# Block-product projection: raw weights in a buffer of their own, weight work ahead of the shaping, three norms first in the conditioning

## What is computed

```python
mod = silu(c) @ w_ada + b_ada              # 1024 x 3072
shift, scale, gate = split(mod, 3)
h = rms_norm(x, norm_g) * (1 + scale) + shift
u = h @ w_in                               # 1024 x 8192
a_q, a_f, a_i, a_g, b_q, b_k, b_v, b_g = split(u)
o_a = rms_norm(hgrn2(a_q, a_f, a_i)) * silu(a_g)
o_b = rms_norm(stick_breaking(b_q, b_k, b_v)) * silu(b_g)
x = x + gate * (concat(o_a, o_b) @ w_out)
return rms_norm(x) * final_g
```

## Time and profile before

| | us |
|---|---|
| median of 3 runs | 3369.33 |
| lowest and highest | 3368.42, 3372.13 |
| the profiled execution | 3368.01 |
| its span, first to last instruction | 3366.2 |
| TensorE busy | 2992.5 (89%) |
| VectorE busy | 1887.7 (56%) |
| ScalarE busy | 1279.8 (38%) |
| GpSimd busy | 615.1 (18%) |
| conditioning | 0 to 107.4 |
| projection, matmuls | 121.8 to 1661.0 |

### The profile page before, as it was taken

How to read it: one execution, slowest core, us unless ns; L and a number is a source line. 1 busy time by engine, 2 the same in 40 slices (tenths; PEclk the granted TensorE clock), 3 DMA queues, 4 the chain that set the end, 5 groups by cost and what they waited for, 6 DMA issues and landing times. The chain is left out here.

```text
span 3366.2 us, 50012 instructions
## 1 busy us (share of the span) xinstructions
PE 2992.5 (89%) x19104; PEld 2509.7 (75%) x19104; DVE 1887.7 (56%) x2013; ACT 1279.8 (38%) x2090; POOL 615.1 (18%) x384
## 2 busy tenths in 40 slices
PE   6687889999687888999888885999999999979998
PEld 4566667777576667878688885887887888868887
DVE  2644334444643334343388884887888878754343
ACT  3422222333323222333211112777777777731111
POOL 0221122222311122222166552000000000000000
PEclk8798899999898898999899997999999999989999
DMA  8124444333323444333344434444243441053220
GB/s 319 38 88 118 129 117 119 97 98 99 108 88 110 131 113 128 100 98 100 122 146 142 135 101 117 111 126 127 51 108 96 126 118 35 14 181 121 79 100 38
DMA packets 277208, 369.72 MB, mean 110 GB/s; under 512 B 13680, under 2 KB 194160, under 8 KB 268272
## 3 DMA queue, kind: packets, MB, share of 16 engines
q1 hardware_dynamic: 276496, 366.03, 35.6%
q10 hardware_dynamic: 480, 0.53, 0.1%
HBM read 244.87 MB, written 121.64 MB: 109 GB/s over the span
## 5 line engine op out<-in xcount | busy, mean ns | idle before, releaser
L470 PE MATMUL b_ps<-hc_hi,w_hi 128*128 128x512 f32 x1792 | 526.9, 418 | 188.9 <-DVE w_lo L581 164.9
L470 PEld LDWEIGHTS b_ps<-hc_hi,w_hi 128*128 128x128 f32 x1792 | 339.6, 198 | 273.9 <-DVE w_lo L581 185.1
L650 DVE TENSOR_TENSOR u<-b_ps,u 128x512 f32<-128x512 f32 x320 | 220.5, 689 | 516.7 <-PE b_ps L470 516.3
L470 PE MATMUL b_ps<-hc_lo,w_hi 128*128 128x512 f32 x1792 | 506.5, 406 | 0.0
L470 PE MATMUL b_ps<-hc_hi,w_lo 128*128 128x512 f32 x1792 | 495.1, 399 | 0.0
L1341 DVE TENSOR_TENSOR_SCAN run<-akeep 128x768 f32<-128x768 f32 (+7 forms) x256 | 414.1, 1660 | 130.4 <-ACT akeep L1311 129.6
L470 PEld LDWEIGHTS b_ps<-hc_lo,w_hi 128*128 128x128 f32 x1792 | 354.4, 198 | 80.0
L470 PEld LDWEIGHTS b_ps<-hc_hi,w_lo 128*128 128x128 f32 x1792 | 349.2, 195 | 78.5
L501 ACT ACTIVATE w_hi<-w_raw 128x1024 fp32r<-128x1024 f32 (+1 forms) x192 | 216.0, 1190 | 409.8 <-POOL w_raw L320 409.8
L1300 ACT ACTIVATE wt<-t_ps 128x512 f32<-128x512 f32 (+3 forms) x640 | 313.5, 534 | 143.6 <-PE t_ps L1230 143.4
L1230 PE MATMUL t_ps<-ident,run 128*128 128x128 f32 x2176 | 311.5, 278 | 7.7 <-DVE run L1341 7.0
(11 more groups left out here) (151 smaller groups left out, 3514.4 us busy)
## 6 DMA issues: line engine op xcount, KB each, us to landing
w_raw<-in_w_in SPq DMA_DIRECT2D x128, 512.0 KB, 4.8
aq<-s_qhi SPq DMA_DIRECT2D x64, 256.0 KB, 6.1
aq<-s_qlo SPq DMA_DIRECT2D x64, 256.0 KB, 6.6
o<-s_o SPq DMA_DIRECT2D x16, 1024.0 KB, 5.9
ada<-in_w_ada SPq DMA_DIRECT2D x12, 1024.0 KB, 9.1
xg<-in_x SPq DMA_DIRECT2D x4, 2048.0 KB, 12.7
s_gq<-u SPq DMA_DIRECT2D x32, 256.0 KB, 2.5
s_gf<-u SPq DMA_DIRECT2D x32, 256.0 KB, 2.5
```

The source lines that it names most:

```text
L470: mm = nc.tensor.matmul(bank[:, :], wt[:, n % 2, j, k * P:(k + 1) * P], ht[:, j, k * 512:(k + 1) * 512], start=(j < 4 and c == 0), stop=(c ...
L650: nc.vector.tensor_tensor(dst, bank[:, :], add, ALU.add).then_inc(sum_ready, 1)
```

## The change

The raw weights get a buffer of their own, `w_raw` with four quarters, filled by one transfer of 1 MB; it is single, and its load for tile n waits until the three rests of tile n-1 are made. The seven-piece slots (`w_sum`, still in the bytes of `w_lo`) only take GpSimd's four sums. The load is two tiles ahead in SP's list: `load_w(n + 2)` stands before the stores of tile n. The pieces are cut anew, as 0, 1 to 4 and 5 to 6, and their order of rounding is 0, 5 to 6, 1 to 4; the first and last wait for the load alone. ScalarE rounds right behind the evacuation, between the turned copies; VectorE computes the three rests between bank sums 1, 2 and 3, and the first shape now stands before bank sum 4.

In the conditioning three groups are squared before the first `high`, two modulation tiles each are multiplied behind groups 2 and 3, and the loads of the last two stand behind all stores of `h`. Work of tile 0 moves ahead of the barrier: the rounding and rest of the first operand of `h`, the rounding of all three weight pieces and their rests. For this, x and the first two modulation buffers are shifted in memory, and the third gets bytes of its own.

```diff
 # conditioning: SP
-                sp.dma_start(w_raw[:, 0, 0:3:2], io["w_in"][0][:, 0:2]).then_inc(w_first, 16)
-                sp.dma_start(w_raw[:, 0, 5:7], io["w_in"][0][:, 2:4]).then_inc(w_first, 16)
+                sp.dma_start(pt["w_raw"][:, :, :], io["w_in"][0]).then_inc(pt["w_loaded"], 16)
                 load_ada(n_mod)
                 load_ada(n_mod + 1)
                 store_h(0)
                 load_x(3)
+                store_h(1)
                 load_ada(n_mod + 2)
                 load_ada(n_mod + 3)
-                store_h(1)
 # conditioning: TensorE, behind the transposes of group g
-                    modulation(n_mod + g)
+                    if g >= 2:
+                        modulation(n_mod + 2 * (g - 2))
+                        modulation(n_mod + 2 * (g - 2) + 1)
 # conditioning: ScalarE
-                squares(0)
-                squares(1)
+                for g in range(3):
+                    squares(g)
                 act.wait_ge(col_ready, 1)
-                for g in range(TG):
-                    high(g)
-                    if 1 <= g < TG - 1:
-                        squares(g + 1)
+                high(0)
+                high(1)
+                squares(3)
+                high(2)
+                act.wait_ge(hi_ready, 2 * KD + KH)
+                nc.scalar.activation(pt["hc_hi"][:, 0], raw[:, 1], ACT.Copy).then_inc(pt["h_high"], 1)
+                for piece in (0, 2, 1):
+                    round_w(nc, act, pt, 0, piece)
+                high(3)
 # conditioning: VectorE
-                for g in range(TG):
-                    if 1 <= g < TG - 1:
-                        norm(g + 1)
-                    take_mod(n_mod + g)
+                norm(2)
+                norm(3)
+                for n in range(n_mod, n_mod + 2):
+                    take_mod(n)
+                for piece in range(3):
+                    rest_w(nc, dve, pt, 0, piece)
+                for n in range(n_mod + 2, n_ada):
+                    take_mod(n)
 # conditioning: GpSimd
-                combine_w(nc, pool, w_raw, t_done, 0)
+                combine_w(nc, pool, pt, 0)
+                first_rest(nc, pool, pt, 0)
...
+def combine_w(nc, pool, pt, n):
+    raw, t, done = pt["w_raw"], pt["w_sum"][:, n % 2], pt["t_done"]
+    pool.wait_ge(pt["w_loaded"], 16 * (n + 1))
+    if n >= 2:
+        pool.wait_ge(pt["u_ready"], 7 * (n - 1))
+    nc.gpsimd.tensor_tensor(t[:, 3], raw[:, 1], raw[:, 0], ALU.subtract).then_inc(done, 1)
...
+W_PIECES = [(0, 1), (1, 5), (5, 7)]
+W_ROUND = {0: 1, 2: 2, 1: 3}
...
+def round_w(nc, act, pt, n, piece):
+    a, b = W_PIECES[piece]
+    if piece == 1:
+        act.wait_ge(pt["t_done"], 4 * (n + 1))
+    else:
+        act.wait_ge(pt["w_loaded"], 16 * (n + 1))
+    if n >= 2:
+        act.wait_ge(pt["u_ready"], 7 * (n - 1))
+    nc.scalar.activation(pt["w_hi"][:, n % 2, a:b], w_source(pt, n, piece), ACT.Copy).then_inc(pt["w_high"], 1)
+
+def rest_w(nc, dve, pt, n, piece):
+    a, b = W_PIECES[piece]
+    dve.wait_ge(pt["w_high"], 3 * n + W_ROUND[piece])
+    if piece != 1:
+        dve.wait_ge(pt["t_done"], 4 * (n + 1))
+    if n >= 2:
+        dve.wait_ge(pt["u_ready"], 7 * (n - 1))
+    nc.vector.tensor_tensor(pt["w_lo"][:, n % 2, a:b], w_source(pt, n, piece), pt["w_hi"][:, n % 2, a:b].bitcast(F32),
+                            ALU.subtract).then_inc(pt["w_split"], 1)
+
+def first_rest(nc, pool, pt, p):
+    pool.wait_ge(pt["h_high"], 7 * p + 1)
+    nc.gpsimd.tensor_tensor(pt["hc_lo"][:, 0], pt["h_raw"][:, 1], pt["hc_hi"][:, 0].bitcast(F32),
+                            ALU.subtract).then_inc(pt["h_first"], 1)
...
 # projection: ScalarE, tile n
+                    back = n >= 1 and not feature(n - 1)
                     act.wait_ge(u_ready, 7 * n + 1)
                     wait_free(act, n, 1)
                     nc.scalar.activation(s_buf[1][:, n % 2, :], b1[n % 2][:, :], ACT.Copy).then_inc(one_ready, 1)
-                    if n >= 1 and not feature(n - 1):
-                        for q in range(4):
-                            turned(n - 1, q)
                     if n + 1 < NT:
-                        w_rounded(n + 1)
+                        round_w(nc, act, pt, n + 1, 0)
+                        round_w(nc, act, pt, n + 1, 2)
+                    if back:
+                        turned(n - 1, 0)
+                    if n + 1 < NT:
+                        round_w(nc, act, pt, n + 1, 1)
                     if n == NCH - 1:
                         h_rounded(1, 0)
-                    for q in range(4):
+                    if back:
+                        turned(n - 1, 1)
+                        turned(n - 1, 2)
+                    shape(n, 0)
+                    if back:
+                        turned(n - 1, 3)
+                    for q in range(1, 4):
                         shape(n, q)
 # projection: VectorE, tile n
                     summed(n, 0)
+                    if n + 1 < NT:
+                        rest_w(nc, dve, pt, n + 1, 0)
                     summed(n, 1)
+                    if n + 1 < NT:
+                        rest_w(nc, dve, pt, n + 1, 1)
                     summed(n, 2)
+                    if n + 1 < NT:
+                        rest_w(nc, dve, pt, n + 1, 2)
+                    shape(n, 0)
                     summed(n, 3)
-                    shape(n, 0)
-                    if n + 1 < NT:
-                        w_rest(n + 1, 0)
-                        w_rest(n + 1, 1)
                     shape(n, 1)
                     shape(n, 2)
-                    if n + 1 < NT:
-                        w_rest(n + 1, 2)
                     summed(n, 4)
                     shape(n, 3)
 # projection: SP
                 def load_w(n):
-                    if n >= 2:
-                        sp.wait_ge(u_ready, 7 * (n - 1))
-                    src = io["w_in"][n % NCH]
-                    sp.dma_start(w_raw[:, n % 2, 0:3:2], src[:, 0:2]).then_inc(w_in_sem[n % 2], 16)
-                    sp.dma_start(w_raw[:, n % 2, 5:7], src[:, 2:4]).then_inc(w_in_sem[n % 2], 16)
+                    sp.wait_ge(w_split, 3 * n)
+                    sp.dma_start(w_raw[:, :, :], io["w_in"][n % NCH]).then_inc(w_in_sem, 16)
...
+                load_w(1)
                 for n in range(NT):
-                    if n + 1 < NT:
-                        load_w(n + 1)
+                    if n + 2 < NT:
+                        load_w(n + 2)
```

77 lines of the change are left out of this document (31 added, 46 removed).

## The result

| | before, us | after, us |
|---|---|---|
| median of four runs each, side by side | 3368.88 | 3163.63 |
| lowest and highest | 3364.97, 3372.13 | 3162.22, 3164.05 |
| span of the profiled execution | 3366.2 | 3162.3 |
| TensorE, VectorE, GpSimd busy | 2992.5, 1887.7, 615.1 | 2928.2, 1906.7, 628.2 |

A forecast was written before the change was run, and what follows sets the result against it. Row tiles were taken to stall on weights started too late, above floors of 19.04 and 21.02 us. From 3368.0, -19.2 - 102.9 + 2.1 - 106.0 gives 3142.0; plus 1.3 for the median, stated 3143, range 3130 to 3190.

The forecast's parts named there:

- Bound and gain: Tiles 1 to 30 and 33 to 63: row tiles, stored unturned, stop waiting for weights; -102.9 and -106.0 us.
- Load, sums, rounding, rests: Next tile's weights: load 5.2 us, GpSimd's sums done at 5.5, rests at 13.3, counted (T) from a tile's first product.
- Shaping, "costed at nothing, covered by PE": Tile's end: last shape, behind load and stores, ends 4 to 5 us into the next tile; 0, uncovered up to 3 us.
- gates late: Rival, 16%: ScalarE waits for stores behind the load in 24 gf, sq and sk tiles; +40 at most, 3183.
- The ring: Gate buffer, rest to rest: load, store, shapes, bank sum, evacuation, rounding and rests take 20.7 us, about a tile's length.
- Loop, 16.8 us, and the clash: Weights, load to load: 16.8 us, or 18.8 with VectorE's shapes slowed beside GpSimd's sums, under the 19.04 floor.
- At most two short shapes: VectorE beside GpSimd's sums: at most two shapes per tile slowed, 2 x 0.99, about 2 us; sum unchanged.
- the row's price: VectorE operation of 2048 columns with two SBUF inputs: 2.29 us alone, 3.28 beside GpSimd, so 0.99 more per clash.
- no run here shows the full price yet: VectorE and GpSimd clash: the skill's rule would cost up to a quarter of 5.3 us each; loop 19.5, total 3157.
- Conditioning: Before projection: earlier squares and stores start it near 95.2 instead of 107.43; with tile 0 at 41.9, tile 1 -19.2 us.
- Change of halves: Tiles 31 and 32: h lands late behind the load, PE stands before its fourth transpose; 79.1 us in all, +2.1.
- SP first waits for the rests (T = 14.4): Tile 31: SP issues tile 33's load 14.4 us after the first product, h's reload behind it; h lands near 23.

The follow-up runs named there:

- the nine profiles: Profiles of nine kernels that have the new conditioning, the changed kernel's included; tile 1 starts at 135.8 to 138.3 us in them.

## Why the prediction was right or wrong

The time lies in the range, and of the 226 us forecast 205 came. Inside this one step was wrong and the others held.

**Bound and gain.** The reading that row tiles lost a quarter of their time to weights asked for too late was right: the early load, with its buffer, gives 3214 without the new orders. The forecast took load and orders for one; it did not see that the orders alone cost time. Its old times are those of a turned tile, T = 0.2 for the load and 5.4 for GpSimd; in the row tile of the earlier trace rows, which starts at 176.74, the load went out at T = 6.3, behind stores, and GpSimd began at T = 11.7, not "about 6". No term of the sum rests on this.

**Load, sums, rounding, rests** hold to 0.3 us where no ring binds: the next load is issued at T = 13.0 where 13.3 was worked out. The load's duration was sized at 5.2 us and measured 5.9 in the median; in the ten tiles off the floor GpSimd started 5.3 to 8.0 us after the issue.

**Shaping, "costed at nothing, covered by PE", is the step that failed.** What happened is the mechanism of the rival "gates late", with its size off in two places. The ring binds in the forget gate's tiles and not in the square kinds' (12.9 us, where the rival had 24 tiles at up to 1.7), and the turned copies have such a ring too, on which no term was set (7.0 us in four tiles). Together 19.9 us in these ten tiles; and the ring of the copies reaches tile 31 as well, see the change of halves. By stage the forecast misses +1.2, +19.9 with 0.3 of rounding, +3.1 and -2.2: that the ten tiles alone come to nearly the 20.6 us it was low by is in part luck, as the start and the unchanged code behind happen to cancel most of the rest. The rival's time, 3183 at most, would have been as far off on the other side. The runs with stores ahead of the load in just these tiles take back all of it in the turned tiles and the larger part in the forget gate's, to 3131.3 with the change of halves.

**Loop, 16.8 us, and the clash.** "At most two short shapes" meet GpSimd at 0.99 us each; two forget-gate operations grow by 1.07 and 0.97, so the row's price held. The longest clash shows that it has no such ceiling: a rest of 1.22 us became 5.03 beside a GpSimd operation of 4.91, in the run with the reloads of h first. The Trainium skill (SBUF — State Buffer, "Who interferes with whom") says that the later of the two blocks for the whole instruction, and that `tensor_scalar` can clash as well; these traces agree, with 5.03 us and with 1.56 us for an operation that takes 0.49 alone. The prediction's "no run here shows the full price yet" has its run now.

**Conditioning** came out almost term by term: high(1) ended at 67.2 (66.6), high(2) at 77.6 (77.7), the roundings at 82.7 (83.1), high(3) at 90.6 (89.6), the modulations at 95.5 (94.3), and the projection began at 96.4 (95.2). Tile 0 took 41.9 us, as worked out from tile 32 of before. Tile 1 at 137.1 lies inside the 135.8 to 138.3 of the nine profiles. Taken back one at a time, the late squares cost 3.9 to 5.6 us at tile 1 and the early weights 7.1.

**Change of halves.** The mechanism was right, PE before its fourth transpose behind h behind the load. The step "SP first waits for the rests (T = 14.4)" is right for a turned tile that nothing has delayed, 13.9 in tiles 17 to 20 and 25 to 28; in tile 31 the load went out at T = 18.8. From there everything is 4 us late, and h's sums begin at 40.5 instead of 36.4; the 42.7 us behind them were 41.7. The delay is the same failed step again, the ring of the turned copies: with stores first in the tiles ahead, and tile 31's own order kept, the load went out at 13.9, h's sums began at 34.7 and the two tiles took 76.1 us, under the 79.1 forecast.

What stays open: why the square kinds lose when their first stores go ahead of the load and the forget gate's gain; whether a larger gate buffer would remove both, which was not tried; and how much of the harm of the orders alone is the wait of the first rest for all four sums.

## What to carry to other kernels

When a load is moved forward in time, look at what it is now queued ahead of: a 1 MB load before 256 KB stores makes every buffer that waits for such a store as slow as the load, and each buffer needs its own ring written out, the small ones of two slots above all. An earlier load and an order that uses it are one change: test the two corners before crediting either. A ring that is 1.5 us longer than a tile costs nothing for some tiles, while it eats the slack: follow an issue time from tile to tile, not only in one. And a wait that is removed from a chain shows only what stands next in it, so follow the chain to the end of the stage before pricing the gain.

## What the runs showed of the hardware

VectorE's 128x1024 rest took 5.03 us beside a 128x2048 GpSimd operation of 4.91 us and ended 1.09 us behind it, where 1.22 is its own time (the run with the reloads of h first). The clash works both ways: GpSimd's 128x512 sums, 1.29 us alone, took 3.27 us beside VectorE's operations of 2048 columns (the run with GpSimd's sums held back). A store of 256 KB from the gate buffer landed in 3.3 us in the median; a store asked for right behind the 1 MB load landed after 8.0 us in tile 23, and ScalarE had stood idle for 12.4 us by then.
